# Gated DeltaNet chunk inverse: 16 by 16 diagonal blocks by substitution on VectorE instead of three doubling levels on TensorE

## The reference

```python
CHUNK = 64
kk = jnp.einsum('bhnid,bhnjd->bhnij', k, k)
a = jnp.where(strict, beta[..., :, None] * kk * decay, 0.0)     # strictly lower, 64 x 64
rhs = jnp.concatenate([beta[..., None] * v, (beta * jnp.exp(gc))[..., None] * k], axis=-1)
sol = lax.linalg.triangular_solve(eye + a, rhs, left_side=True, lower=True, unit_diagonal=True)
u_bar, w = sol[..., :dv], sol[..., dv:]
```

## Time and profile before

| | |
|---|---|
| runs | 2263.19, 2266.43, 2272.91 us |
| profiled execution | span 2262.2 us; it has no other time of its own, and the fastest run is 1.0 us above this span |
| PE busy | 2195.8 us, 97% of the span |
| PEld, DVE, ACT, POOL busy | 81%, 49%, 42%, 31% |
| granted TensorE clock | 0.992 of full |
| the chain that ended last | PE 87%, ACT 3%, DVE 3%, DMA 2% |
| pieces of heads 0 to 7 | from about 694 to 1340 us, one head in 80.5 us |

### The profile page before, as it was taken

How to read it: one execution, slowest core, us unless ns; L and a number is a source line. 1 busy time by engine, 2 the same in 40 slices (tenths; PEclk the granted TensorE clock), 3 DMA queues, 4 the chain that set the end, 5 groups by cost and what they waited for, 6 DMA issues and landing times.

```text
span 2262.2 us, 30759 instructions
## 1 busy us (share of the span) xinstructions
PE 2195.8 (97%) x11040; PEld 1827.7 (81%) x11040; DVE 1117.9 (49%) x1559; ACT 939.4 (42%) x1647; POOL 693.5 (31%) x529
## 2 busy tenths in 40 slices
PE   6899999999999999999999999999999999999998
PEld 5688787887887888888888887888788888878887
DVE  7522422323247656656756534424866666650044
ACT  5544343443445556555655542123533333320013
POOL 6786556556532111111111114331000000043240
PEclk8999999999999999999999999999999999999999
DMA  5111312313142102211211334251222222261221
GB/s 133 49 47 47 98 53 67 93 47 85 57 107 72 59 16 74 65 37 46 65 54 39 131 140 130 65 137 31 66 83 80 80 82 83 84 230 49 67 83 75
DMA packets 251922, 175.66 MB, mean 78 GB/s; under 512 B 41448, under 2 KB 225960, under 8 KB 251840
## 3 DMA queue, kind: packets, MB, share of 16 engines
q1 hardware_dynamic: 221776, 136.46, 20.7%
q10 hardware_dynamic: 30064, 38.10, 5.2%
HBM read 143.36 MB, written 31.18 MB: 77 GB/s over the span
## 4 chain that ended last, share of the span: by engine, by line
PE 87%; ACT 3%; DVE 3%; issue 3%; DMA 2%; POOL 1%; ACTq 1%; POOLq 1%; DVEq 0%; SPq 0%
PE bank L213 19%; PE bank L2263 17%; PE bank L1064 16%; PE bank L2504 10%; PE bank L1273 6%; PE bank L1523 2%; PE bank L1506 2%; PE bank L689 1%; PE bank L2279 1%; PE bank L1513 1%; PE bank L700 1%; PE bank L1560 1%; PE bank L1555 1%; PE bank L1556 1%; PE bank L1561 1%
## 5 line engine op out<-in xcount | busy, mean ns | idle before, releaser
L213 PE MATMUL bank<-u_hi,w_hi 128*128 128x512 f32 x704 | 311.2, 442 | 6.2 <-ACT z_next L1742 4.9
L199 POOL CAST w_hi<-raw 128x1024 fp32r<-128x1024 f32 (+1 forms) x60 | 61.7, 1028 | 715.1 <-PE bank L213 500.5
L213 PE MATMUL bank<-u_hi,w_lo 128*128 128x512 f32 x704 | 276.9, 393 | 0.0
L213 PE MATMUL bank<-u_lo,w_hi 128*128 128x512 f32 x704 | 276.3, 392 | 0.0
L2485 POOL CAST dn_hi<-dn_raw 128x896 fp32r<-128x896 f32 (+1 forms) x24 | 25.3, 1053 | 565.6 <-DMA dn_raw<-in_w_down 460.2
L213 PEld LDWEIGHTS bank<-u_hi,w_lo 128*128 128x128 f32 x704 | 132.4, 188 | 29.3
L201 POOL TENSOR_TENSOR w_lo<-raw,w_hi 128x1024 fp32r<-128x1024 f32 (+1 forms) x60 | 149.3, 2489 | 8.6
L213 PEld LDWEIGHTS bank<-u_hi,w_hi 128*128 128x128 f32 x704 | 133.7, 190 | 22.2 <-ACT z_next L1742 5.3
L213 PEld LDWEIGHTS bank<-u_lo,w_hi 128*128 128x128 f32 x704 | 134.0, 190 | 15.0 <-issue 1.9
L941 POOL TENSOR_TENSOR q_lo_s<-q_sum_s,q_hi_s 128x512 fp32r<-128x512 f32 x92 | 122.6, 1338 | 64.9 <-ACT q_hi_s L996 59.3
L1810 DVE SCALAR_TENSOR_TENSOR conv_out<-conv_in,conv_c,conv_out 128x1024 f32<-128x1024 f32 (+1 forms) x96 | 100.3, 1045 | 14.9 <-issue 12.0
(11 more groups left out here) (433 smaller groups left out, 5918.8 us busy)
## 6 DMA issues: line engine op xcount, KB each, us to landing
raw<-in_w_in SPq DMA_DIRECT2D x36, 512.0 KB, 3.9
raw_first<-in_w_in SPq DMA_DIRECT2D x24, 512.0 KB, 3.9
raw_second<-in_w_in SPq DMA_DIRECT2D x24, 512.0 KB, 4.7
row<-scr_rows ACTq DMA_DIRECT2D x24, 512.0 KB, 4.6
raw_gate<-in_w_gate SPq DMA_DIRECT2D x22, 512.0 KB, 3.9
raw_up<-in_w_up SPq DMA_DIRECT2D x22, 512.0 KB, 3.9
scr_v<-gate_out SPq DMA_DIRECT2D x44, 256.0 KB, 2.1
tmp<-scr_gate ACTq DMA_DIRECT2D x16, 512.0 KB, 3.6
```

The source lines that it names most:

```text
L199: nc.gpsimd.tensor_copy(hi[:, 0:kt, :], raw[slot][:, 0:kt, :])
L213: last = nc.tensor.matmul(bank[dst][:, :], wpart[slot][wp][:, k, :], rhs[ap][:, k, half * HALF:(half + 1) * HALF], start=k == 0 and (wp, a ...
```

## The change

For each head the inverse now starts from 16 x 16 diagonal blocks instead of 2 x 2 ones. The pieces `t0` and the levels 1, 2 and 3 are gone on TensorE, ScalarE and VectorE. In their place VectorE, right behind its `kk1` piece at step 17, runs `inverse_blocks`: it moves the 64 blocks of 16 x 16 (8 chunks, 8 blocks each) so that each of the 128 partitions holds one block, or a half of a pair that a mask picks (four 32 x 32 block transposes), inverts them by forward substitution (15 columns, a multiplication and an addition each, with a drain before each), spreads them again, and moves them back with four transposes into `inv`, which ScalarE has set to zero behind the scan of the head before. Level 4 follows at step 32, where level 1 stood at step 22. The steps of the later pieces move by one, the taps of i = 0 move from 20, 23, 25, 28 to 35, 36, 38, 39, those of i = 1 from 34, 37, 40, 43 to 41, 43, 45, 46, and those of i = 2 by one. A mask multiplication per head (L1786) goes, and POOL builds three masks instead of seven, and a small one more.

```diff
-        STEPS_AT = {..., 17: ["kk1"], 18: ["qk0"],
-                    19: ["qk1", "t00"], 20: ["t01"], 41: ["tt0", "tt1"], 43: ["ub0", "ub1", "wt0", "wt1"],
-                    62: ["os"], 63: ["on"]}
-        for level in range(1, 7):
-            STEPS_AT[22 + 3 * (level - 1)] = [f"y{level}"]
...
+        STEPS_AT = {..., 17: ["kk1", "inv"], 18: ["qk0"],
+                    19: ["qk1"], 42: ["tt0", "tt1"], 44: ["ub0", "ub1", "wt0", "wt1"],
+                    63: ["os", "on"]}
+        for level in range(FIRST_LEVEL, 7):
+            at_ = 32 + 3 * (level - FIRST_LEVEL)
+            STEPS_AT[at_] = [f"y{level}"]
+            STEPS_AT[at_ + 1] = [f"p{level}"]
+            STEPS_AT[at_ + 2] = [f"d{level}0", f"d{level}1"]
...
-        TAPS_AT = {20: (0, 0, WHOLE), 23: (0, 1, WHOLE), 25: (0, 2, WHOLE), 28: (0, 3, WHOLE),
-                   34: (1, 0, WHOLE), 37: (1, 1, WHOLE), 40: (1, 2, WHOLE), 43: (1, 3, WHOLE)}
+        TAPS_AT = {35: (0, 0, WHOLE), 36: (0, 1, WHOLE), 38: (0, 2, WHOLE), 39: (0, 3, WHOLE),
+                   41: (1, 0, WHOLE), 43: (1, 1, WHOLE), 45: (1, 2, WHOLE), 46: (1, 3, WHOLE)}
-        SILU_AT = {30: 0, 46: 1, 59: 2}
-        SQUARE_AT = {47: 0, 49: 1}
+        SILU_AT = {41: 0, 48: 1, 60: 2}
+        SQUARE_AT = {49: 0, 51: 1}
-        ROWS_AT, PREPARE_AT = 60, 62
+        ROWS_AT, PREPARE_AT = 61, 62
...
             elif step[0] == "y":
                 level = int(step[1])
+                n = h * 6 + 2 * (level - FIRST_LEVEL)
+                if level == FIRST_LEVEL:
+                    pe.wait_ge(dl["base"], h + 1)
...
+        def quadrant(t, g):
+            first = 32 * min(g, 2)
+            return t[32 * g:32 * g + 32, :].rearrange("p (c t) -> p c t", t=P)[:, :, first:first + 64].rearrange(
+                "p c (e i) -> p i e c", i=BASE)
+
+        def inverse_blocks(dve):
+            v = nc.vector
+            v.memset(x_now[:, :, :], 0.0)
+            for g in range(4):
+                v.transpose(turned[32 * g:32 * g + 32, :, :, :].rearrange("p i m k -> p (i m k)"), quadrant(neg_a, g))
+            dve.drain()
+            v.memset(x_now[:, :, :].rearrange("p i j -> p (i j)")[:, 0:BASE * BASE:BASE + 1], 1.0)
+            v.scalar_tensor_tensor(factor[:, :, :], turned[:, :, 0, :], sub_mask[:, 0:1], turned[:, :, 1, :],
+                                   ALU.mult, ALU.add)
+            for k in range(BASE - 1):
+                shape = [P, BASE - 1 - k, k + 1]
+                more = x_more[:, 0:shape[1] * shape[2]].rearrange("p (i j) -> p i j", j=k + 1)
+                dve.drain()
+                v.tensor_tensor(more, factor[:, k + 1:BASE, k:k + 1].broadcast_to(shape),
+                                x_now[:, k:k + 1, 0:k + 1].broadcast_to(shape), ALU.mult)
+                dve.drain()
+                rest = x_now[:, k + 1:BASE, 0:k + 1]
+                v.tensor_tensor(rest, rest, more, ALU.add)
+            dve.drain()
+            v.tensor_tensor(spread[:, :, :, :], x_now[:, :, :].rearrange("p i j -> p j i").unsqueeze(2).broadcast_to(
+                                [P, BASE, 2, BASE]),
+                            sub_mask[:, :].unsqueeze(1).unsqueeze(3).broadcast_to([P, BASE, 2, BASE]), ALU.mult)
+            dve.drain()
+            for g in range(4):
+                last = v.transpose(quadrant(inv, g), spread[32 * g:32 * g + 32, :, :, :].rearrange("p j m i -> p (j m i)"))
+            last.then_inc(dl["base"], 1)
+            dve.drain()
+            v.tensor_copy(by_block(inv_right[:, :], FIRST_LEVEL), side_columns(inv[:, :], FIRST_LEVEL, 1)).then_inc(dl["ir"], 1)
...
                 v.tensor_tensor(neg_a[:, hs], bank[Y0 + half][:, :], neg_a[:, hs], ALU.mult).then_inc(dl["a"], 1)
-                dve.drain()
-                v.copy_predicated(c4(inv_t, half), merge_mask[:, 0:1, :].broadcast_to([P, 4, P]),
-                                  c4(neg_a, half)).then_inc(dl["t0t"], 1)
+            elif step == "inv":
+                dve.drain()
+                wait(dve, dl["blank"], h)
+                inverse_blocks(dve)
```

More of the change, by code:

```diff
@@ L1487, in delta_pe @@
                 last.then_inc(dl["qk"], 1)
[L1488 to L1493, removed]
-                last.then_inc(dl["t0"], 1)
             elif step[0] == "y":
                 level = int(step[1])
-                n = h * 12 + 2 * (level - 1)
-                if level == 1:
-                    pe.wait_ge(dl["t0c"], two + 2)
-                    pe.wait_ge(dl["a"], two + 2)
-                pe.wait_ge(dl["ar"], h * 6 + level)
+                n = h * 6 + 2 * (level - FIRST_LEVEL)
+                if level == FIRST_LEVEL:
+                    pe.wait_ge(dl["base"], h + 1)
+                pe.wait_ge(dl["ar"], h * 3 + (level - FIRST_LEVEL + 1))
                 for q in range(NCH // 2):
-                    if level > 1 and q % 2 == 0:
+                    if level > FIRST_LEVEL and q % 2 == 0:
                         pe.wait_ge(dl["dtm"], n + (q // 2 - 1))
@@ L1598, in delta_act @@
                 act.wait_ge(dl["a"], two + 2)
[L1599 to L1608 removed]
+                f(by_block(a_right[:, :], FIRST_LEVEL), side_columns(neg_a[:, :], FIRST_LEVEL, 1),
+                  ACT.Copy).then_inc(dl["ar"], 1)
             elif step[0] == "y":
                 level = int(step[1])
[L1611 removed]
+                act.wait_ge(dl["y"], h * 3 + (level - FIRST_LEVEL + 1))
                 y_now = bank[Y0][:, :].rearrange("p (q j) -> p q j", j=P)
@@ L1636, in delta_act @@
                 f(o_sq[:, half * HALF:(half + 1) * HALF], bank[Y0 + half][:, :], ACT.Square).then_inc(dl["osq"], 1)
+                if half == 1 and not isinstance(h, int):
+                    f(inv[:, :].rearrange("p (c t) -> p c t", t=P), ident[:, :].unsqueeze(1).broadcast_to([P, NCH, P]),
+                      ACT.Copy, scale=0.0).then_inc(dl["blank"], 1)
             elif step == "on":
@@ L1695, in delta_vec @@
                                   side_columns(inv[:, :], level + 1, 1)).then_inc(dl["ir"], 1)
-            elif step == "t01":
-                dve.wait_ge(dl["t0c"], two + 2)
-                v.tensor_copy(by_block(inv_right[:, :], 1), side_columns(inv[:, :], 1, 1)).then_inc(dl["ir"], 1)
             elif step[:2] == "wt":
```

82 lines of the change are left out of this document (41 added, 41 removed).

## The result

| | before | after |
|---|---|---|
| median of the runs (least to most) | 2266.59 us (2263.19 to 2272.91) | 2330.52 us (2326.60 to 2331.84) |
| profiled execution, span | 2262.2 us | 2328.6 us |
| PE busy | 2195.8 us, 97% | 2153.5 us, 92% |
| DVE busy | 49% | 52% |
| granted TensorE clock | 0.992 | 0.970 |

The change makes the kernel 2.75% slower: the ratio is 1.0275 (95% interval 1.026 to 1.029), 64 us where 46 had been forecast. Half of the inverse left TensorE, and TensorE now stands idle for longer than that work took.

The account below looks back on a forecast made before the run. TensorE was taken to set the time, with VectorE's chain too late for `y4`. Seven heads at +4.6 (32.2), head 7 12.3 and iteration 0 5.6 make +50 us on 2263: 2313, forecast 2312, range 2250 to 2348.

Parts of the forecast that it names:

- How long VectorE has: From the second `kk` product on `neg_a` (869.5) to TensorE reaching `y4` (880.8): 11.3 us for VectorE's chain.
- POOL: 3.2: POOL's weight-tile split beside `y4` blocks VectorE's two-SBUF-input operations: 3.2 us added, nothing to 3.5 possible.
- The clock: Behind each 9.0 us wait TensorE runs about 3.5 us at 1.2 instead of 2.4 GHz: 1.7 us lost a head.
- (a): Taps of i = 0 end at step 39, delaying ScalarE's copies: TensorE waits 1.5 us (0 to 2) at `d6`, seven heads.
- (b): Last tap of i = 1 stands between `a0` and `b0` at step 46: 0.5 us, in seven heads.
- (d): Iteration h = 0: late taps run in series on the path, its end 5.6 us later (3 to 8).
- (e): Head 7, `delta_end`: attention-branch loads behind the later `qdec` make `y5` wait 8.0 us, plus 1.7 clock; head total +12.3.
- the transpose that costs twice the contiguous operation: Rival: a hop at every element makes a transpose 1.36 us, chain 4.1 us longer, 2345 us; chance 0.14.
- That POOL doesn't block: Rival: strides cost as forecast without POOL blocking, `y4` waits 5.8 us, 2287 us; chance 0.12.
- The faster rival: Transposes at contiguous rate, POOL not blocking: `y4` waits 2.9 us, too little for the clock to fall, 2251; chance 0.10.
- The full gain: Rival: VectorE is in time for `y4`, 8 heads give 65 us, 2200 us; chance 0.04.
- the smaller gain: The faster rival's case, 2251 us, deciding from a wait of 4.5 us at `y4`; chance 0.10.

Follow-up runs that it names:

- the run with the fillers: Changed kernel with 40 matmuls, whose result nobody reads, ahead of TensorE's wait at `y4`: 2316.59 us, ratio 1.0229.
- the schedule alone: Kernel before, inverse still on TensorE, with taps, silu and squares at the changed kernel's steps and pieces one step later: 2292.68 us, ratio 1.0118.
- the kernel with 8 by 8 blocks: Changed kernel with substitution on 8 by 8 blocks, levels 3 to 6 on TensorE from step 29, taps and branch splits moved: 2243.56 us, ratio 0.9898.

## Why the prediction held, and where it was off

The direction, the place and the mechanism were as forecast: 2312 us, with 2250 to 2348 as the range, against 2330.5. The 18 us between them are more than the noise, and two errors worked against the rest: POOL's share and the branch's wait had been put too high. By its own steps:

- **What leaves TensorE: 8.1 us a head.** Without the columns 7.9 are seen. Held, 0.2 too high.
- **How long VectorE has: 11.3 us.** Measured 11.3.
- **The thirty dependent operations: 8.0.** From 892.25 to 903.28 are 11.0 us, less 2.65 for POOL is 8.4. They start 0.25 to 0.30 us apart, as the slope from the earlier trace rows gave it.
- **The eight transposes: 7.2 (0.9 each).** 8.4, 1.04 each. The bounds of 0.6 to 1.15 held the value; the middle between them was too low. The upper one had been worked out from another engine's strided write, and the value lay much nearer to it. The rate of the Trainium skill that the prediction named beside the sum, and kept out of it, would have given 1.0 to 1.4.
- **Spreading 0.9, memsets and `factor` 0.8:** 1.2 and 1.1, with their drains.
- **POOL: 3.2.** 2.65: what a blocked operation loses is POOL's duration less the part that was over when it began, and less its own. The cast blocks as well (0.67 us), which no row of before had shown. The Trainium skill's rule (SBUF — State Buffer, Who interferes with whom) said so, and the trace agrees with it; by the same section a copy in a two-port mode takes part too, and 2.40 against 0.43 us for `inv_right` agree with that.
- **The wait at `y4`: 9.0.** 10.5, from 21.7 us of chain instead of 20.1. This is the largest part of what was missed: 8 x 1.5 = 12 us.
- **The clock: 1.7 a head.** 2.0, by the run with the fillers: 2 to 3 us in eight heads. The earlier trace rows had been read at a wait of 4.9 us, with 3.5 us at the lower clock behind it; behind these waits it is 3.3 and 5.5 us in turn, of which half would be 2.2 us in the mean.
- **(a) 1.5 at `d6`, (b) 0.5 at `a1`:** 1.6 and 0.3, shown by the schedule alone as well as by the change.
- **(d) iteration 0: 5.6.** 5.1, and back to 0 with the old steps. Held.
- **(e) head 7: 12.3.** 13.7: the branch costs 6.1 + 0.7 instead of 8.0, and the clock, `y4` again more.
- **Not in the sum:** 2.7 us in the feed-forward part.

Seven heads at -7.9 + 10.5 + 2.0 + 1.6 + 0.3 = +6.5 are 45.5 us where 32.2 stood; with 13.7 + 5.1 + 2.7 - 0.8 that is 66.2, and the spans differ by 66.4. Of the 1.6 us by which the chain was too short in the sum, the transposes make 1.2, the columns 0.4, and spreading, memsets and `factor` 0.6, less 0.55 for POOL. So the term that fell short most is that of the transposes; the clock's and that of TensorE's work follow with 0.3 and 0.2 us a head.

Of the rivals, the transpose that costs twice the contiguous operation (2345) came near by its size; its premise of 1.36 us was too much, for the contiguous one is 0.70 and the strided one half as much again. That POOL doesn't block (2287) is refuted by the run with POOL held back. The faster rival (2251) took a wait of 2.9 us to be too short for the clock to fall. The kernel before had shown otherwise, in its feed-forward part:

```profile
1998.51 0.47 PE L2263 MATMUL bank<-t_hi_t,p_hi_d 128*128 128x512 f32 x1 [2.87 <-DVE up_out L2325]
```

```profile
2000.00:2002.00 2.00, 2.00 (x6) 1.55 (x5) 2.00 (x2) 0.00 (x0) 0.00 (x0) 0.50 1.04 414
```

TensorE had short gaps ahead of that wait as well (1.65 of 2 us busy over 1994 to 1996), and no run has a single wait of 2.9 us in the heads, so what it would have cost there stays open. Behind the 1.6 us at `y3` in the kernel with 8 by 8 blocks the clock stays at 1.00. The full gain and the smaller gain needed a chain of under 11.3 and under 16 us, and it takes 19.0 even without POOL.

## What to carry to other kernels

Work that goes from the engine that sets the time to another one gains only if the other's chain is shorter than the time between its input and the place where its result is wanted. So write both down first: here 11.3 us against 19 to 22, which eats the 7.9 us of gain; with blocks of half the side the chain is 10.7 us and the kernel gets 1.6% faster. Whether 16 by 16 blocks could pay with `y4` many more steps later, and the scan pushed back with it, was not tried. A wait on TensorE then costs more than its length, because the clock goes down with it, and a step put in a new place must be looked at against the other engine's fixed work (POOL's split) and against loads which a semaphore of the moved piece sets free.

## What the runs showed of the hardware

- A VectorE transpose of 512 float32 elements a partition takes 0.70 us on adjacent words and 1.04 when either side hops at each element; one of 256 elements with the hop 0.63.
- A single VectorE copy of 512 float32 elements with one input (0.43 us) is held by POOL as an operation with two inputs is: it takes 2.40 us and ends 0.3 us behind POOL's operation of 2.37 us. The prediction had thought of operations with two inputs only; it cost 6.6 us in the schedule alone and as much again in the first kernel with 8 by 8 blocks.
- The clock fell 3.6 us into a wait of 10.5 us in one head and 2.4 us into it in the next (0.95 over 900 to 902; 0.79 over 986 to 988, with the wait from 984.8). It came back 3.3 and 5.5 us behind the first matmul, so the same wait cost about 1.7 or 2.7 us more; by the run with the fillers it was 2.0 in the mean.
